# A layer's second output projection computed as three products of rounded and remaining parts

## The reference

```python
y = head_layernorm(y_f + y_b, p['ln_w'].reshape(HC, NC), p['ln_b'].reshape(HC, NC), WKV_LN_EPS)
y = y + jnp.sum(r * k * p['r_k'], axis=-1, keepdims=True) * v
oc = y.reshape(b, L, HC * NC) * g                 # 512 channels: tiles 0 to 3
...
od = rmsnorm((yd_f + yd_b).reshape(b, L, D_INNER) * jax.nn.silu(zg), p['gnorm'])   # tiles 4 to 7
merged = jnp.concatenate([oc, od], axis=-1)
return merged @ p['w_out'], (S_f, S_b, H_f, H_b)
```

## Time and profile before

| | |
|---|---|
| median of 3 runs | 2125.38 us (2121.13 to 2132.78) |
| the profiled execution | 2123.67 us |
| its span in the trace | 2121.9 us |
| TensorE busy | 2007.5 us, 95% |
| VectorE busy | 1120.2 us, 53% |
| ScalarE busy | 687.4 us, 32% |
| GpSimd busy | 152.7 us, 7% |
| stage `post_*` up to unit 2 of the projection | 1540.3 to 1581.3 us |
| units 2 and 3 | 1581.3 to 1598.7 us |
| from unit 4 to the first `ffn_up` result read by ScalarE | 1598.7 to 1654.2 us |

### The profile page before, as it was taken

The page is one execution under the profiler, slowest core; times in us unless marked ns, Lnnn a source line. Parts: engine busy times, 40 slices in busy tenths (PEclk is TensorE's granted clock), DMA queues, the critical chain, the costliest instruction groups (busy, mean ns, idle before and its releaser), DMA issues.

```text
span 2121.9 us, 41446 instructions
## 1 busy us (share of the span) xinstructions
PE 2007.5 (95%) x18452; PEld 1766.6 (83%) x18452; DVE 1120.2 (53%) x2004; ACT 687.4 (32%) x1229; POOL 152.7 (7%) x145
## 2 busy tenths in 40 slices
PE   5998999999999999989989689999999999999998
PEld 3785445999999999989985478888856999999997
DVE  3236754465555452344546467777654655556323
ACT  3223554343333241232434433332112433334211
POOL 2000000000000000000006421221000000000000
PEclk8999999999999999999988799999999999999999
DMA  9025737122221132221200000000022122222222
GB/s 344 28 80 183 264 131 266 40 80 80 80 73 60 54 82 70 61 92 61 80 30 23 6 2 4 3 4 3 4 85 80 44 77 80 80 80 55 75 63 77
DMA packets 141506, 163.74 MB, mean 77 GB/s; under 512 B 2368, under 2 KB 106864, under 8 KB 141328
## 3 DMA queue, kind: packets, MB, share of 16 engines
q1 hardware_dynamic: 137872, 148.81, 21.5%
q0 software_dynamic: 3456, 12.28, 1.7%
HBM read 157.32 MB, written 3.75 MB: 76 GB/s over the span
## 4 chain that ended last, share of the span: by engine, by line
PE 86%; DVE 8%; DMA 3%; ACT 2%; issue 1%; POOL 0%; ACTq 0%; SPq 0%; DVEq 0%; POOLq 0%
PE ps L220 81%; DMA ring<-in_ada_w 1%; PE ps L1843 1%; DVE work L2384 1%; DMA ring<-in_ffn_up 1%; PE ps L1222 1%; DVE work L492 1%; DVE small L1357 1%; DVE x_lo_r L498 0%; DMA ring<-in_l_w_out 0%; DVE work L2429 0%; ACT work L1286 0%; PE ps L2161 0%; PE ps L2143 0%; PE ps L456 0%
## 5 line engine op out<-in xcount | busy, mean ns | idle before, releaser
L220 PE MATMUL ps<-x_hi_r,w_lo 128*128 128x320 f32 (+3 forms) x2240 | 522.5, 308 | 3.8 <-ACTq L204 2.9
L220 PE MATMUL ps<-x_lo_r,w_hi 128*128 128x320 f32 (+2 forms) x1792 | 427.4, 309 | 11.6 <-DVE g_lo L842 8.2
L220 PE MATMUL ps<-x_hi_r,w_hi 128*128 128x320 f32 (+2 forms) x1792 | 430.2, 311 | 0.9 <-issue 0.9
L220 PE MATMUL ps<-work 64*64 64x64 f32 (+7 forms) x4942 | 352.0, 266 | 37.5 <-ACT work L2304 9.2
L220 PEld LDWEIGHTS ps<-x_hi_r,w_lo 128*128 128x128 f32 (+1 forms) x2240 | 374.2, 187 | 6.0 <-ACTq L204 3.1
L220 PEld LDWEIGHTS ps<-work 64*64 64x64 f32 (+4 forms) x4942 | 231.5, 147 | 142.6 <-issue 83.2
L220 PEld LDWEIGHTS ps<-x_lo_r,w_hi 128*128 128x128 f32 x1792 | 307.4, 189 | 12.5 <-DVE g_lo L842 8.7
L220 PEld LDWEIGHTS ps<-x_hi_r,w_hi 128*128 128x128 f32 x1792 | 304.8, 188 | 1.4 <-issue 1.3
L672 DVE SCALAR_TENSOR_TENSOR work<-ps,par,work 128x511 f32<-128x511 f32 (+1 forms) x188 | 103.3, 549 | 267.3 <-ACT work L807 259.7
L720 DVE TENSOR_TENSOR w_lo<-ring,w_hi 128x1024 fp32r<-128x1024 f32 (+1 forms) x152 | 158.4, 1077 | 97.2 <-ACT w_hi L709 96.8
L807 ACT ACTIVATE work<-ps,par 128x640 f32<-128x640 f32 x88 | 77.9, 886 | 392.8 <-PE ps L220 392.8
(11 more groups left out here) (352 smaller groups left out, 2450.1 us busy)
## 6 DMA issues: line engine op xcount, KB each, us to landing
ring<-in_ada_w SPq DMA_DIRECT2D x24, 2048.0 KB, 7.9
ring<-in_ffn_up SPq DMA_DIRECT2D x44, 1024.0 KB, 7.0
ring<-in_ffn_down SPq DMA_DIRECT2D x16, 1408.0 KB, 6.8
ring<-in_l_w_in SPq DMA_DIRECT2D x11, 1024.0 KB, 5.0
ring<-in_l_w_out SPq DMA_DIRECT2D x4, 2048.0 KB, 8.3
ring<-in_l_w_in SPq DMA_DIRECT2D x3, 2048.0 KB, 9.5
h<-in_xT POOLq DMA_DIRECT2D x1, 2560.0 KB, 14.7
out_yT<-work POOLq DMA_DIRECT2D x2, 768.0 KB, 4.4
```

The source lines that it names most:

```text
L220: return pe.matmul(out, lhsT, rhs, start=first, stop=last)
```

## The change

- Layer 1's output projection is computed as three products, as layer 0's is: `wout0_pe` and `wout_pe` become one function, and `wout_act` and `wout_dve` split block 1's weights beside units 0 and 1 in both layers.
- In the stage `post_*`, ScalarE rounds each of the eight input tiles (`post_hi_act`) and the four parts of block 0's weights; VectorE forms the rests (`post_lo_dve`, `out_w_lo`). The order is written out: tiles 4, 5 and weight part 2 ahead of the loop; behind job 0 part 3 and tiles 6, 7; behind job 1 part 0 and tile 0; behind job 2 part 1 and tile 1; tiles 2 and 3 at the end. The rests overwrite `merged` in place; the rounded parts have new room in `work`.
- Each piece of `unit` in `post_pe` waits for its weight part and its tile; TensorE's order of work is as before.
- Block 0 is loaded when the seventh recurrent job has read slot 0 of the ring; block 1 still waits for the barrier. For that the recurrence's tables and start states are laid out one half per slot, and the start states come in two loads instead of one.

```diff
+        POST_PARTS, POST_TILES = (2, 3, 0, 1), (4, 5, 6, 7, 0, 1, 2, 3)
+        def post_hi_act(act, t):
+            if t < 4:
+                act.wait_ge(sg("y_gated"), t + 1)
+            if t == 3:
+                act.wait_ge(sg("stored"), SCAN_STORED + 16)
+            act.activation(oh2(t), merged(t), ACT.Copy).then_inc(sg("x_hi"), 1)
+
+        def post_lo_dve(dve, t):
+            dve.wait_ge(sg("x_hi"), out_tiles(2) + POST_TILES.index(t) + 1)
+            dve.tensor_tensor(xh(t), merged(t), oh2(t).bitcast(F32), ALU.subtract).then_inc(sg("x_lo"), 1)
...
                 if 4 in ks:
                     pe.wait_ge(sg("y_centred"), 3 + u)
                     if u == 0:
-                        units["w"] = next_block(pe)
+                        units["w"] = out_block(pe, 1, 0)
                 for k in ks:
-                    if k < 4:
-                        pe.wait_ge(sg("y_gated"), k + 1)
-                    for a, b in SEG:
-                        ins = mm(pe, pair_ap(u, a, b), units["w"][:, k, P * u:P * u + P], merged(k, a, b), k == 4, k == 3)
+                    pe.wait_ge(sg("w_lo"), out_parts(1) + POST_PARTS.index(k // 2) + 1)
+                    pe.wait_ge(sg("x_lo"), out_tiles(2) + POST_TILES.index(k) + 1)
+                    for w, x in ((wh, oh2), (wh, xh), (wl, oh2)):
+                        for a, b in HALF:
+                            ins = mm(pe, spair(u, a, b), w[:, k, c:c + P], x(k, a, b), k == 4 and w is wh and x is oh2,
+                                     k == 3 and w is wl)
...
+            post_hi_act(act, 4)
+            post_hi_act(act, 5)
             square(0)
+            out_w_hi(act, 1, 0, 2, True)
...
+                if j == 0:
+                    out_w_hi(act, 1, 0, 3)
+                    post_hi_act(act, 6)
+                    post_hi_act(act, 7)
+                elif j < 3:
+                    out_w_hi(act, 1, 0, j - 1)
+                    post_hi_act(act, j - 1)
+            post_hi_act(act, 2)
+            post_hi_act(act, 3)
...
+            post_lo_dve(dve, 4)
+            post_lo_dve(dve, 5)
+            out_w_lo(dve, 1, 0, 2)
             for j in range(4):
                 dve.scalar_tensor_tensor(bonus_b[j][:, :], r_(j), pc("r_k", j), k_(j), ALU.mult, ALU.mult)\
                     .then_inc(sg("rk_ready"), 1)
...
                 dve.tensor_tensor(merged(j), merged(j), gates_b[j][:, :], ALU.mult).then_inc(sg("y_gated"), 1)
-            dve.wait_ge(sg("y_gated"), 4)
+                if j == 0:
+                    out_w_lo(dve, 1, 0, 3)
+                    post_lo_dve(dve, 6)
+                    post_lo_dve(dve, 7)
+                elif j < 3:
+                    out_w_lo(dve, 1, 0, j - 1)
+                    post_lo_dve(dve, j - 1)
+            post_lo_dve(dve, 2)
+            post_lo_dve(dve, 3)
...
         def wout_act(act, s, shift):
             for u in range(8):
                 res_square(act, s, u)
-                if s == 0 and u < 2:
+                if u < 2:
                     for part in (2 * u, 2 * u + 1):
-                        out_w_hi(act, 1, part)
+                        out_w_hi(act, s // 2, 1, part, part == 0)
...
-                            (s0_b, t_in["wkv0"])))
+                            (s0_b[0], t_in["wkv0"][:, 0:256]), (s0_b[1], t_in["wkv0"][:, 256:512])))
...
                 if n == first_after_wkv:
+                    assert n % RING == 0
+                    sp.wait_ge(sg("wkv_yi"), 2 * (JOBS - 1))
+                if n == first_after_wkv + 1:
                     sp.wait_ge(phase, 4 * WKV_LEFT)
```

More of the change, by code:

```diff
@@ L527, in out_lo_dve, with out_w, out_w_hi @@
             return dve.tensor_tensor(xh(t, a, b), src, xl(t, a, b).bitcast(F32), ALU.subtract)
-        def out_w_hi(act, b, part):
-            n = wout_first[0] + b
-            if part == 0:
+        def out_w(l, b):
+            return wh_b[:, SLOT * b:SLOT * b + SLOT] if l == 0 else wh2_b[:, SLOT * b:SLOT * b + SLOT]
+        def out_w_hi(act, l, b, part, first=False):
+            n = wout_first[l] + b
+            if first:
                 act.wait_ge(full[n % RING], 16 * parts_before[n % RING][n + 1])
             w = SLOT // WP
-            act.activation(wh_b[:, SLOT * b + w * part:SLOT * b + w * part + w],
+            act.activation(out_w(l, b)[:, w * part:w * part + w],
                            ring[:, SLOT * (n % RING) + w * part:SLOT * (n % RING) + w * part + w], ACT.Copy)\
@@ L538, in out_w_hi, with out_w_lo @@
             w_parts["act"] += 1
-        def out_w_lo(dve, b, part):
-            n = wout_first[0] + b
+        def out_w_lo(dve, l, b, part):
+            n = wout_first[l] + b
             w_parts["dve"] += 1
@@ L546, in out_w_lo, with out_block, wout_pe @@
             dve.tensor_tensor(wl_b[:, at:at + w], ring[:, at:at + w],
-                              wh_b[:, SLOT * b + w * part:SLOT * b + w * part + w].bitcast(F32), ALU.subtract)\
+                              out_w(l, b)[:, w * part:w * part + w].bitcast(F32), ALU.subtract)\
                 .then_inc(sg("w_lo"), 1)
[L550 to L558, removed]
+        def out_block(pe, l, b):
+            n = wout_first[l] + b
+            next_block(pe)
+            k3 = lambda buf: buf.rearrange("p (k c) -> p k c", k=KT)
+            return k3(out_w(l, b)), k3(wl_b[:, SLOT * (n % RING):SLOT * (n % RING) + SLOT])
+        def wout_pe(pe, s, begun=None):
+            l, units = s // 2, res_units(s)
+            w = {0: begun}
+            x_hi = xl if s == 0 else oh2
             def operands(k):
@@ L570, in unit @@
                 c = P * (m % 4)
-                project_split(pe, u % 2, lambda k: wh[:, k, c:c + P], lambda k: wl[:, k, c:c + P], xl, xh, KT, before,
+                project_split(pe, u % 2, lambda k: wh[:, k, c:c + P], lambda k: wl[:, k, c:c + P], x_hi, xh, KT, before,
                               toks=HALF if b - a == NT else ((a, b),), cut=NT // 2 if b - a == NT else CUT)\
                     .then_inc(sg("res_prod"), 1)
[L575 to L605, removed]
+            if begun is None:
+                w[0] = out_block(pe, 0, 0)
+                unit(0, operands)
+                batch_turn(pe, 1)
+                unit(1)
             for u in range(2, 4):
@@ L609, in wout_pe @@
             released.append((sg("res_prod"), RES0[s] + 4))
-            w[1] = next_block(pe)
+            w[1] = out_block(pe, l, 1)
+            pe.wait_ge(sg("w_lo"), out_parts(l) + 2 * WP)
             for u in range(4, 8):
@@ L644, in wout_dve @@
                     res_add(dve, s, u - 1)
-                residual_dve(dve, s, u, gate, early_psum if u >= 4 else spair if s == 0 else pair_ap)
-                if s == 0 and u < 2:
+                residual_dve(dve, s, u, gate, spair if u < 4 else early_psum)
+                if u < 2:
                     for part in (2 * u, 2 * u + 1):
-                        out_w_lo(dve, 1, part)
+                        out_w_lo(dve, s // 2, 1, part)
             part_spread(dve, s, 0, ch)
@@ L683, in build @@
         wl_b = rounded("w_lo", "ring", 0, RING * SLOT)
+        oh2_b, wh2_b = rounded("o_hi", "work", W0, KT * NT), rounded("o_w_hi", "work", W0 + KT * NT, 2 * SLOT)
+        oh2 = lambda t, a=0, b=NT: tile(oh2_b, t, a, b)
         xh_b, xl_b = rounded("x_hi_r", "merged", 0, KT * NT), rounded("x_lo_r", "work", 0, KT * NT)
@@ L1999, in build @@
         SCAN_STORED = 16 * 5
-        s0_b = ring[:, 2 * GSZ:2 * GSZ + 512]
-        assert 2 * GSZ + 512 <= RING * SLOT
+        s0_b = [ring[:, SLOT * half + GSZ:SLOT * half + GSZ + 256] for half in range(2)]
+        assert GSZ + 256 <= SLOT
         en_b, agx_b, km_b = stat[:, 0:650], sqb[:, 0:NT], sqb[:, NT:2 * NT]
```

41 lines of the change are left out of this document (22 added, 19 removed).

## The result

The changed kernel takes 2147.84 us (median of 4 runs, 2145.90 to 2147.98), the kernel before 2125.77 (4 runs, 2121.13 to 2132.78): ratio 1.010, 95% interval 1.0083 to 1.0118. I had predicted 2138.5 in a range of 2127 to 2148: the sign is right, the time lies inside the range by only 0.2 us, and the loss is 22 us where I had 13. The profiled execution took 2147.76 us with a span of 2146.0, 24.1 more than the span before.

What follows compares the result with a forecast made beforehand. TensorE was taken to bound the kernel. Stage order and units 2, 3 (8.3), clock falls (4.8), block 1 and after (0.0) and moved loads (0.3) summed to 13.4 us more, giving 2138.5 us, range 2127 to 2148.

Steps and rivals of the forecast that it cites:

- Parts 1 and 2: Stage `post_*` and units 2, 3: TensorE saves 3.3 us in each, but added VectorE work makes unit 4 8.2 to 8.4 late.
- that rival: Output projection: three products cost three quarters of float32, 0.81 us per k tile, saving another 2 us, 2136; chance 0.05.
- The steps: Stage followed job by job: `turn(0)` 2.3 us late, 4.8 us idle ahead of k = 6 and k = 1, unit 2 11.5 late.
- the order doesn't bite: Stage: rests are formed ahead of TensorE's need, so k = 6 and k = 1 don't wait; 2117 to 2120 us; chance 0.07.
- Part 3: Stage: TensorE's pauses bring two to four half-clock falls of some 1.6 us; three taken, 4.8 us.
- half clock through the stage: Stage: falls join, half clock from `turn(0)` to `gates(1)`, four falls in all; 16.5 us and more, 2142 to 2146; chance 0.15.
- Part 4: Block 1 to first `ffn_up` result: as layer 0's 55.28 us, landing and rounding bind unit 6, so 0.0 us.
- Part 5: Moved loads: block 0's earlier load costs nothing, the start states' second load 0.3 us.
- GpSimd price: Stage before the recurrence: the start states' second load costs 0 to 0.9 us on GpSimd; 0.3 taken.
- One sign: Profile after, end of the stage: unit 2 starts 11 to 17 us later than 1581.3.
- the sum: Whole kernel: 13.4 us added to the profiled 2123.67, with the median before 1.7 higher, giving 2138.5 us.

Runs made afterwards that it cites:

- e1: Changed kernel with block 0's load put back behind the barrier, not under the last recurrent job; 2140.64 us.
- e8: Changed kernel with residuals and squares of units 4 and 5 placed ahead of splitting the first `ffn_up` block, both layers; 2131.90 us, ratio 1.0038.
- e10: Changed kernel with matmuls without use in only the stage's two 4.7 us TensorE pauses, 14 each; 2137.72 us.
- the fills: Changed kernel with matmuls without use in all six TensorE pauses of the stage; 2138.00 us, ratio 1.0062.
- e5: Changed kernel with the stage's same operations in another order on VectorE, ScalarE and TensorE; 2121.90 us, ratio 0.998.
- e6: Reordered kernel (e5) with residuals and squares of units 4 and 5 ahead of splitting the first `ffn_up` block; 2109.67 us, ratio 0.9939.
- e7: e6 with block 0's load issued later, once the last recurrent job's first state step is done; 2111.32 us.
- e9: Kernel before the change with residuals and squares of units 4 and 5 ahead of splitting the first `ffn_up` block; 2118.66 us, ratio 0.997.
- e4: Changed kernel with layer 1's rests of tiles and block 0's weights formed for one column only, products taking rounded parts; 2131.45 us.

## Why the prediction was right in sign and range, and short by 9 us

**Parts 1 and 2, the count at full clock: right.** Units 2 and 3 took 14.03 us, 0.877 per k tile as in layer 0, and gave 3.4 us (3.3). The Trainium skill (FP8 and Floating Point Precision, TensorE Precision Notes) counts four passes for float32, from which I had estimated 0.81 for three; layer 1 too shows 0.877, so that rival is out. The steps: `turn(0)` waited for the spread, k = 6 came after 4.73 us of idle TensorE (4.8), k = 1 after 4.72 (4.8), k = 2 after 2.21 (2.8; it was 2.7 in e1, e8 and e10), and with the clock held up by the fills unit 2 starts 54.4 us after the stage's start, 1.1 of it by the half clock of the means, against a count of 52.4: 0.9 us short. The 65.0 us of the changed kernel are then 52.4 counted, 0.9 that the count lacks, 1.4 in the means and 10.3 by the clock behind the pauses. The rival "the order doesn't bite" fell, and e5 shows that it was the order alone: VectorE's 14.6 spare us in the earlier trace rows could take the rests, but not where they were written.

**Part 3, the clock: the term was mis-sized, 4.8 us for 10.3 in the profiled execution.** I took three falls of 1.6 us each, from two pauses in the earlier trace rows that stood alone in dense work. In the stage, behind the means, there were four: from TensorE's busy time and PEclk, us by us, I estimate that they took 2.5, 1.7, 6.0 and 1.7 us, part of it hidden in waits. Three are near my price, though two of these followed pauses of 0.9 and 2.2 us which I had counted as harmless or halfway so. The fourth is 12 us of half clock without a break from k = 1 to the pause ahead of k = 2, and it varies: TensorE worked through it for 9.5 us in e1 and for 5 in e8. So with the same list the term came to 6.5, 6.9 and 10.3 us in three executions; why the long fall lasts as it does, no run shows. My rival "half clock through the stage" (0.15, 7.9 us of clock) has the four falls and nearly the time, 2146; but PEclk was 1.00 from `turn(0)` to 1560, where it had half clock. The means had a further 1.4 us of half clock, which began before the stage (7.57 us against 6.16 in the kernel before). They took 7.6 us in e6 and 6.1 in e7, with the same list in the stage, so I don't put this down to the change.

**Part 4, the tail: 0.0 for +2.5, and the reason was wrong.** I had written that landing and rounding of the `ffn_up` block bind unit 6. They do only through VectorE's order: e6 and e8 remove the stall with the same landing. I had read layer 0's 55.28 us as a floor because layer 1's was the same; it was one order with its wait in both. Against that template, the block's first rounding began 9.6 us after the issue and not 8.2, so the stall was 4.9 us and not 3.4, and the half clock behind it took 2.9 us and not 1.7 (estimated like the falls above). Its row, in the columns of the earlier trace rows:

```profile
1635.00:1640.00 5.00, 5.00 (x18) 5.00 (x18) 2.33 (x4) 0.52 (x1) 0.00 (x0) 0.56 0.00 0
```

Against layer 1 before, the +2.5 is a gain of 5.2 us by the split, eaten up by 3.1 us more of stall (4.9 against 1.8) and 4.6 us of half clock in two falls, where PEclk had stayed at 1.00: 57.8 less 4.9 and 4.6 is 48.3, as e6 has it with 48.5, and 55.3 less 1.8 is 53.5, as e9 with 53.3. So block 1 as three products was worth some 5 us that its order hid. Why the block came 1.4 us later isn't shown.

**Part 5, the moved loads: 0 for +1.8.** I had looked at who waits for the load and not at what runs beside it. The gap is new in this change, and gone with the load moved (e1, e7). The GpSimd price of 0.3 didn't show: that part of the program came out 0.9 us shorter.

**What was luck.** Sign and main mechanism are mine: the pauses stand where I counted them, and the clock fell behind them. That the time lies inside the range is luck in part: the +2.5 of the tail and the +1.8 of the last job stood in no rival, and the range's end had been set by the half-clock rival and the GpSimd price alone. One sign that I had named didn't come: unit 2 starts 24.9 us later than 1581.3, not 11 to 17. And the sum has a slip: 2123.67 + 13.4 + 1.7 is 2138.8, not 2138.5.

## What to carry to other kernels

Spare time of an engine is worth only what its list lets one use: before adding steps, write down for each step who waits for the one in front of it, and put new steps behind the hand-overs that feed TensorE, or a job ahead. A pause that TensorE gets costs its length and can cost a fall of the clock on top: in this stage 15.2 to 15.8 us of pauses brought another 6.5 to 10.3 us. Where two places show the same time, look for a shared order before taking it for a bound.

## What the hardware showed that I had not expected

- Work without use made the kernel faster: 46 matmuls in the pauses, 10.6 us less in the stage and some 10 us in the whole.
- Like pauses cost differently from one execution to another: stages of 65.0, 60.5 and 60.5 us with pauses of 4.7, 0.9, 4.7 and 2.2 to 2.7 us, and 2.2 to 3.3 around the first piece. A forecast of such a stage has a spread of some 4 us of its own.
- A pause of 0.88 us was followed by half clock (e10, PEclk 0.67 in 1570 to 1575), one of 2.99 us wasn't (e4, PEclk 1.00 in 1580 to 1590).
- A 2 MB load that nobody waits for cost TensorE a gap of 1.1 to 1.9 us, behind an instruction transfer that came 2.5 us late, and nothing once it was issued in a stretch of TensorE with waits of 0.4 us between its matmuls.
